# Expert units of a two-layer diffusion trunk with a mixture of experts: from 56 units (16 whole, 24 pairs, 16 spare) to 58 (14 whole, 25 pairs, 19 spare)

## The reference

```python
scores = jax.nn.sigmoid((h @ p['w_router']).astype(jnp.float32))
biased = scores + p['router_bias']
# 4 of 8 groups are kept by the sum of their two best; then the 8 best experts of these
_, eidx = lax.top_k(jnp.where(emask, biased, -jnp.inf), TOP_K)
w = take_along_axis(scores, eidx); w = w / sum(w) * 2.5
hg, hu = einsum('td,edf->tef', h, w_gate), einsum('td,edf->tef', h, w_up)
act = jax.nn.silu(hg) * hu * gates[:, :, None]
routed = jnp.einsum('tef,efd->td', act, p['w_down'])
```

## Time and profile before

| | us |
|---|---|
| median of 3 runs | 1696.32 |
| lowest, highest | 1692.69, 1702.27 |
| profiled execution | 1706.42 |
| its span, first to last instruction | 1704.6 |
| PE busy (matmul) | 1406.1 (82%) |
| DVE, ACT, POOL busy | 671.4, 408.3, 256.3 |

### The profile page before, as it was taken

How to read it: one execution, slowest core, us unless ns; L and a number is a source line. 1 busy time by engine, 2 the same in 40 slices (tenths; PEclk the granted TensorE clock), 3 DMA queues, 4 the chain that set the end, 5 groups by cost and what they waited for, 6 DMA issues and landing times.

```text
span 1704.6 us, 23713 instructions
## 1 busy us (share of the span) xinstructions
PE 1406.1 (82%) x8772; PEld 962.6 (56%) x8772; DVE 671.4 (39%) x1382; ACT 408.3 (24%) x788; POOL 256.3 (15%) x273
## 2 busy tenths in 40 slices
PE   4799687986999999997059996888889999999942
PEld 2598465954555555554028875676655555555521
DVE  4422767153332222222743347633523222222246
ACT  2324425021222222221013344321112122222201
POOL 1000000001322222231010000000023232322200
PEclk9799857977999999999579996699889999999975
DMA  9553202126988888885874412122469888888853
GB/s 319 206 183 118 105 31 109 50 87 233 362 305 317 328 333 324 305 332 181 340 257 173 141 70 99 41 99 99 180 252 358 333 313 307 324 294 298 328 207 154
DMA packets 126098, 378.96 MB, mean 222 GB/s; under 512 B 28224, under 2 KB 33152, under 8 KB 122784
## 3 DMA queue, kind: packets, MB, share of 16 engines
q1 hardware_dynamic: 86976, 291.31, 46.2%
q0 software_dynamic: 35552, 60.97, 10.1%
q10 hardware_dynamic: 3456, 25.17, 3.6%
HBM read 480.36 MB, written 64.75 MB: 320 GB/s over the span
## 4 chain that ended last, share of the span: by engine, by line
PE 71%; DVE 16%; DMA 6%; issue 4%; ACT 2%; SPq 0%; DVEq 0%; ACTq 0%; POOLq 0%
PE bank L1143 25%; PE bank L1158 11%; PE bank L1129 7%; PE bank L1050 5%; PE bank L771 4%; PE bank L772 4%; PE bank L773 4%; DVE aT L1843 4%; DMA ring<-in_w_ada 3%; DVE aT L1580 1%; PE bank L1066 1%; DMA ring<-in_w_in 1%; PE bank L790 1%; PE bank L1114 1%; PE bank L976 1%
## 5 line engine op out<-in xcount | busy, mean ns | idle before, releaser
L1143 PE MATMUL bank<-slab,xT 128*64 128x256 f32 x2112 | 301.5, 396 | 20.6 <-issue 20.5
L1143 PEld LDWEIGHTS bank<-slab,xT 128*64 128x64 f32 x2112 | 180.6, 142 | 104.2 <-issue 38.2
L732 POOL DMA_INDIRECT sums_scratch<-h,row_table x112 | 112.8, 1007 | 538.6 <-PE bank L1129 438.4
L1826 DVE TENSOR_TENSOR work<-work,bank 128x128 f32<-128x128 f32 x112 | 32.3, 288 | 399.1 <-ACT work L1405 399.1
L1143 PE MATMUL bank<-ring,xT 128*64 128x256 f32 x960 | 152.7, 392 | 9.6 <-issue 9.6
L1158 PE MATMUL bank<-slab,work 128*64 128x512 f32 x528 | 147.3, 592 | 1.5 <-DVE work L1832 1.5
L1405 ACT ACTIVATE work<-bank 128x128 f32<-128x128 f32 x112 | 31.1, 278 | 457.5 <-PE bank L1143 457.5
L1815 DVE COPY h<-bank 128x512 f32<-128x512 f32 x112 | 77.5, 692 | 127.0 <-PE bank L1158 127.0
L1143 PEld LDWEIGHTS bank<-ring,xT 128*64 128x64 f32 x960 | 90.1, 140 | 44.8 <-issue 14.8
L1143 PE MATMUL bank<-h_hi_slot,xT 128*64 128x256 f32 x512 | 108.5, 396 | 6.4 <-issue 6.4
L1492 DVE TENSOR_TENSOR w_lo<-ring,w_hi 128x2048 fp32r<-128x2048 f32 x24 | 55.0, 2292 | 122.3 <-ACT w_hi L1229 122.3
(11 more groups left out here) (334 smaller groups left out, 2324.9 us busy)
## 6 DMA issues: line engine op xcount, KB each, us to landing
slab<-in_w_gate SPq DMA_DIRECT2D x112, 512.0 KB
slab<-in_w_up SPq DMA_DIRECT2D x112, 512.0 KB
slab<-in_w_down SPq DMA_DIRECT2D x112, 512.0 KB
ring<-in_w_ada SPq DMA_DIRECT2D x24, 2048.0 KB
ring<-in_w_gate SPq DMA_DIRECT2D x52, 512.0 KB
ring<-in_w_up SPq DMA_DIRECT2D x52, 512.0 KB
ring<-in_w_down SPq DMA_DIRECT2D x52, 512.0 KB
slab<-sums_scratch ACTq DMA_DIRECT2D x24, 1024.0 KB, 11.5
```

Of the source, the lines that this page charges most:

```text
L732: pool.indirect_dma_start(sums_dram, bass.IndirectOffsetOnAxis(ap=row_table[:, u:u + 1], axis=0), y_rows[:, n % 3, :], None, bounds_check= ...
L1143: last = mm(bk[r, 0:2 * P].rearrange("p (k f) -> p k f", k=2), xT[:, n % 2, j, r], w[:, j, :, :], start=(j == 0), stop=(j == NJ - 1))
```

## The change

The numbers of whole, paired and spare units become 14, 25 and 19. Unit order is no longer eight equal turns, but a list that keeps the three kinds in step with their shares, never puts two spare units side by side but for the end of the list, starts with pair, whole, pair, pair, spare, pair and ends with a spare unit. The numbers 16 in the table of overflow windows become `SPARE`.

```diff
-NUNITS = 56
-WHOLE = 16
-PAIRED = 24
-NXW = 32
+NUNITS = 58
+WHOLE = 14
+PAIRED = 25
+SPARE = NUNITS - WHOLE - PAIRED
+NXW = 2 * SPARE
@@
-        for turn in range(8):
-            for kind in ("pair", "whole", "pair", "spare", "pair", "whole", "spare"):
-                u = UNITS_BY_KIND[kind].pop(0)
-                owners = {"whole": [u], "pair": [u, u + PAIRED], "spare": [E + u - WHOLE - PAIRED, E + u - WHOLE - PAIRED + 16]}[kind]
...
+        kinds = ["pair", "whole", "pair", "pair", "spare", "pair"]
+        total = {kind: len(units) for kind, units in UNITS_BY_KIND.items()}
+        while len(kinds) < NUNITS - 1:
+            late = {k: (total[k] - (k == "spare")) * (len(kinds) + 1) / (NUNITS - 1) - kinds.count(k) for k in total}
+            kinds.append(max((k for k in total if k != "spare" or kinds[-1] != k), key=late.get))
+        for kind in kinds + ["spare"]:
+            u = UNITS_BY_KIND[kind].pop(0)
+            owners = {"whole": [u], "pair": [u, u + PAIRED], "spare": [E + u - WHOLE - PAIRED, E + u - WHOLE - PAIRED + SPARE]}[kind]
...
+        assert all(w < E for _, w in loads[:XSLOT])
@@
-                after(ts(place[:, :, :], over_b[:, :, :], 16.0, float(WIN - 16 * P), ALU.is_ge, ALU.mult))
+                after(ts(place[:, :, :], over_b[:, :, :], float(SPARE), float(WIN - SPARE * P), ALU.is_ge, ALU.mult))
```

More of the change, by code:

```diff
@@ L527, in trunk_program @@
         loads, loads_of_unit = [], []
-        for turn in range(8):
-            for kind in ("pair", "whole", "pair", "spare", "pair", "whole", "spare"):
-                u = UNITS_BY_KIND[kind].pop(0)
-                owners = {"whole": [u], "pair": [u, u + PAIRED], "spare": [E + u - WHOLE - PAIRED, E + u - WHOLE - PAIRED + 16]}[kind]
-                loads_of_unit.append([len(loads) + i for i in range(len(owners))] * (2 if kind == "whole" else 1))
-                loads += [(len(order_of_units), w) for w in owners]
-                order_of_units.append(u)
+        kinds = ["pair", "whole", "pair", "pair", "spare", "pair"]
[6 more added lines that the diff above has]
+            owners = {"whole": [u], "pair": [u, u + PAIRED], "spare": [E + u - WHOLE - PAIRED, E + u - WHOLE - PAIRED + SPARE]}[kind]
+            loads_of_unit.append([len(loads) + i for i in range(len(owners))] * (2 if kind == "whole" else 1))
+            loads += [(len(order_of_units), w) for w in owners]
+            order_of_units.append(u)
+        assert all(w < E for _, w in loads[:XSLOT])
         assert sorted(order_of_units) == list(range(NUNITS)) and len(loads) == E + NXW
```

## The result

The changed kernel takes 1745.7 us (median of 3 runs, 1745.4 to 1746.5) against 1696.3 us before: a ratio of 1.029, 95% interval 1.024 to 1.034. That is 49 us more; 33 were forecast.

What follows compares the result with a forecast made beforehand. PE was taken to bound both expert loops, with weight loads nearly a bound too; 25.8 + 3.8 + 0 + 3.0 + 0.5 = 33.1 us on the median 1696.3 gave 1729.4, rounded to 1730, range 1713 to 1748.

Steps and rivals of the forecast that it cites:

- Two more units: In each expert loop, two added units at 6.45 us of PE each: 25.8 us more over both loops.
- Weights moved: Weight queue of both layers: no new overflow, so 64 loads per layer and 291 MB in all, as before.
- the rival of an overflowing expert: An expert overflows its window, so its spare load moves 1.573 MB and joins a chain: 1740 us, chance 0.02.
- Waits of the new order: PE waiting for weights before up products: 20.2 us a loop against 18.3, 3.8 us more in all.
- the recurrence: Unit-by-unit calculation of PE starts, slot releases and load landings in both loops, giving 20.2 us of waits a loop after.
- d: Time a queued weight load lands after the load ahead of it in the loops, taken as 5.15 us.
- the rival of the loads as the bound: Pairs behind pairs or late pairs wait and slow the clock: +8 and +6 us per loop, 1754 us, chance 0.12.
- Slow clock: Up products at lower clock after waits in the loops: no change from 18 us, bounds 6 us either way.
- Start of the loop: First gathers share engines with two more real loads: 1.5 us per layer, 3.0 in all, bounds 0 and 7.9.
- The sign that the prediction asked for: First transposes of the loop start 1 to 2 us later after the gather's issue than the 6.9 us of before.
- Base: Starting time for the sum: the median of 1696.3 us, with the profiled execution of 1706.4 lying 10.1 us above it.
- the even spread pays for the units: Both loops lose their waits and slow clocks, 54.6 us, against 25.8 + 3.5 added: 1671 us, chance 0.04.

Runs made afterwards that it cites:

- The number alone: Kernel before with two more spare units per loop behind its old order, 58 units: 1723.3 us, ratio 1.016 to the kernel before.
- the kernel without waits: Kernel before with its scatters limited to row 0 and the weighted sum reading w_ada instead: 1645.9 us, ratio 0.969 to the kernel before.
- the order alone: Kernel before with its 56 units (16 whole, 24 pairs, 16 spare) ordered by the change's rule: 1689.6 us beside 1695.2, ratio 0.997.
- the third experiment: Changed kernel with its 58 units in another order, chosen so that no chain of loads is late: 1695.9 us beside 1695.2 before, ratio 1.001.

## Why the prediction was right, and where it was short

The direction, the mechanism and the range held: slower, by two units on a loop that PE bounds and by waits for weights. That 1745.7 us lies inside the range is a near thing: the forecast's own upper end, 1746, allowed 14 us of waits, 6 of clock and 4 of the start, and the waits alone came to 15.0, which a smaller start (1.6 for 4) made up for. Term by term, with the mean of two profiles on either side (the changed loops are 802.0 us, those of before 755.9, 46.1 apart):

- *Two more units*: forecast 25.8. The number alone gave 28 us in its median (17 to 38), in the run whose waits stayed, and units whose weights are there still start 6.45 us apart. Right.
- *Weights moved*: 291.31 MB in both. Right; the rival of an overflowing expert is out.
- *Waits of the new order*: forecast 3.8 us more, measured 15.0 (50.4 against 35.4). This is the step that was mis-sized. All six places that the recurrence gave (5, 16, 25, 32, 41, 48) are there, at 1.7, 4.8, 4.2, 3.1, 3.1 and 2.3 us in the first loop for 1.4, four times 3.8 and 2.5: 19.1 us for 19.1. What it missed are units 19, 28, 35 and 44, all with four full gathers and scatters beside loads that have no slack, with 4.9 us in the first loop and 6.6 in the second, where it had 0.1 each. In the first loop the six places thus hit their sum, with single ones about 1 us off; in the second they sum to 17.8. The failing assumption is that d is one number. It was fitted to the groups of five loads of the old order, in which the spare units lie regularly between the full ones. The prediction had named the right doubt (d ran up to 7 us where scatters lay beside it) and put it with the rival of the loads as the bound. That rival gave 1754 us; the truth lies between it and the forecast.
- *Slow clock*: forecast no change, measured 5.3 us more in the mean of two (21.0 against 15.7). The two profiles of before differ by 7.4 us in this term alone, so its size is uncertain. That it hangs on the waits is shown at one end: in the kernel without waits it is nothing, and with 10 to 18 us of waits it is 2 to 4 us.
- *Start of the loop*: forecast 1.5 us a layer. From the first gather's issue to the first up product it takes 10.2 to 11.8 us in the eight loops with two skipped loads among the first seven, mean 11.1, and 11.7 to 12.2 in the twelve with seven real ones, mean 12.0. So 0.8 us. The extra time lies at the second gather, as argued: in the changed kernel PE stops 0.58 us between the transposes of units 0 and 1, which it did not before. The sign that the prediction asked for, first transposes 1 to 2 us later, is not borne out: they start 7.5 to 7.7 us after the gather's issue in the two profiles of the changed kernel, for 6.9 and 6.4 in the first profile of the kernel before, but the six other loops with two skipped loads have 7.4 to 7.8.

```profile
408.62 1.97 PE L1135 MATMUL bank<-consts,big 128*128 128x128 f32 x8 [8.90 <-DMA big<-rows_scratch,token_table]
411.17 1.74 PE L1135 MATMUL bank<-consts,big 128*128 128x128 f32 x8 [0.58 <-DMA big<-rows_scratch,token_table]
```

  Here gathers share the engines with two loads, and the second is late by about a microsecond and not by the 7.9 us that the loads need. The two loads were issued before the first gather (396.15 and 398.19, the gather at 401.13), but their last packets end at 413.7 and 420.0, after both gathers are in: the gathers passed them. That agrees with what the Trainium skill says ("DMA: Bandwidth & Descriptors", Queues, rings and completion order): each engine goes round between the queues that have work.
- *Base*: the sum was made on a profiled execution that lay 10 us above the median, and put on the median unaltered. Of the 13 us between the two profiles of before 7 are slow clock and 2 are waits in the loops, and the other 4 lie outside the loops, so what the kernel before loses there in its usual execution was read too large. The median of the change is therefore further from the median of before (49 us) than profile from profile (39 us).

Of the rivals, the one that ends faster (the even spread pays for the units) failed at its own condition: the rule of the change for the order alone saves 5.6 us in the medians, within the noise. Half of it holds for another order: with the same 58 units in the third experiment the waits saved paid for the units, 1695.9 beside 1695.2 us, but no more than that.

What stays open: why the slow clock cost 12.0 us in one execution of the kernel before, 19.4 in another and 9.9 with the order alone, with nearly the same waits (34.2, 36.5 and 33.2); and how the price of a load splits between gathers and scatters beside it.

## What to carry to other kernels

When two engines are both near their limit, the order of the work decides how many of the slack microseconds are lost: here the same units and bytes took 1746 or 1696 us. Work the order through, load by load over the lookahead of the buffers, so that no load comes late, and count the bytes of all queues there, loads and scatters together; the two orders chosen in this way had 16 and 18 us of waits for 50 and 35. A rule that spreads each kind of unit evenly by itself didn't do that here. And fit a queue's price in a recurrence only for the mix of traffic that it is then used for.

## What the runs showed of the hardware

- The scatters move 25 MB in the two layers and cost the kernel before 57 us in the medians (46 and 56 us of its loops, by profile), though no wait in its loops is put down to the end of a scatter: without them PE is busy all through both loops.
- A load inside the loop cost 5.15 us in the groups of before, but ahead of a loop, alone on the engines at 399 GB/s, 3.9 us. Without scatters a group of five loads is in 24.7 us after its first issue; with them it let PE go after 28.8.
- After waits of 2 to 3 us the up product took 3.67 us in some cases and about 5.3 in others (a granted clock of 0.69 in the one after the wait of 2.8 us at unit 51 of the first profile, a mix of the 2.4 and the 1.2 GHz level); after the waits over 4 us it took 5.0 to 6.5 us each time. Without waits the granted clock was 1.00 for both loops.
- A conditional load that moves nothing costs SP three issues of 0.07 to 0.09 us and no bytes, but it holds one of the seven slots in turn like any other.
